# Router of a mixture-of-experts step: three of five row-tile shifts moved from VectorE to GpSimd

## The chip, the cores and the metric

The kernel runs on one core of one Trainium2 chip. The metric is the device time of one execution in microseconds (us); lower is better. A launch is one program on that one core, and nothing is shared with other cores.

## The reference, cut to what matters

One trunk layer is computed for 640 tokens (128 of context, 512 latent) with D_MODEL = 1024: modulated norm, one wide input projection, an RG-LRU and an attention branch, a merge, a gated residual, and then the part around which this case turns, the mixture of experts:

```
h = rms_norm(x, norm_g[1]) * (1 + sc2) + sh2            # sh2: the shift, one row for context, one for latent tokens
scores = sigmoid(h @ w_router)                          # 640 x 16
sel    = scores + router_bias, in 4 groups of 4
group  = argmax over groups of (sum of the group's two best)
idx    = the two best experts of that group;  w = their scores, normed to sum 1
y      = sum over the two experts e of w_e * (silu(h @ Wg[e]) * (h @ Wu[e])) @ Wd[e]
x      = x + g2 * y
```

## The kernel before, in words

**Stages.** The profile has three of them that matter here. Up to about 785 us TensorE works through 80 weight tiles of the projections. From there to about 816 us lies the router. From 816 us to about 1130 us the experts run, then a short tail adds the rows up, norms and stores them. Matrix products are made in three passes (high times high, high times low, low times high parts of fp32 values), which is why every weight has a Hi and a Lo tile.

**The router stage.** The modulated rows exist as columns in `xa` (channel by token) without the shift. They are needed twice. The logits come from products with the router's weights, with the shift's share added afterwards. The rows themselves are turned by TensorE (`to_rows`, L1048, forty 128x128 transposes in ten groups of four), evicted by ScalarE with the factor of the norm (`rows`, L1473) into `hrow`, five tiles of 128 tokens x 1024 channels, and then the shift row is added in place: `shifted(t)` on VectorE, L2006, one instruction of 128x1024 fp32 for each tile. `shb` holds the two shift rows spread over all partitions; SP loads it beforehand (semaphore `h2_pre`). SP writes each shifted tile to DRAM (`h2d`, called h_rows in the trace, L580), in order of t, each after its own wait for `slot_ok`, and right behind them on the same queue comes the load of the gate weights of expert 1.

**The order of VectorE's work.** It is written out by hand. VectorE makes the ranks (`pair_eq`, `pair_gt`, `in_rank`), the group choice (`gscore`, `r5`, `gtmp`, `ing`), the one-hot `ohsH` for TensorE (L2032), then positions, and at last `ohP` and `ohV` (L2083, L2085), from which TensorE makes the list of tokens of each slot (`idxI`, L2088). Between small instructions that depend on each other the five additions are placed as fill: tiles 0 and 1 after `top2` (L2008), tiles 2 and 3 after the first maximum of the group scores (L2019), tile 4 after the one-hot planes (L2035). `seq.last()` is a wait of VectorE for its own previous instruction.

**Who needs the results.** TensorE waits for `ohsH` at L1057, makes ranks across tokens, turns the residual rows of `x1` (`to_rows(1, ...)`, first four groups before the token list, six after it), and waits for all their evictions (`tr_ev`) before the first expert. ScalarE evicts those rows into `x1t` (L1475); between group four and five it makes the high part of the first up weights. GpSimd waits for `idxI` and for all five DRAM writes (`hrow_out`), then gathers the rows of the first expert tiles by an indirect DMA (L675). `x1t` and `shb` share memory: the last two tiles of `x1t` lie where `shb` lay.

**GpSimd.** Up to about 772 us it makes the low parts of the projection weights (L639, 128x1024, two inputs from SBUF); then it makes two small constants, and nothing more until the gathers. In the tail it multiplies three of the five tiles of summed rows by the gate (`gated`, L713).

Of the kernel before, what the change touches and what calls it, by code (L numbers as in the profile page):

```python
# [22 lines left out]
ALU = mybir.AluOpType  # L23
# [9 lines left out]
TT = T // P  # L33
# [73 lines left out]
HIGH_AT = (0, 3, 7, 11)  # L107
OUT_BANK = (2, 6, 4, 0, 2)
GATED_DVE = 2
ADA_ORDER = (4, 5, 6, 7, 0, 1, 2, 3)  # L110
SPANS = ((0, 0, NP), (1, NP, T))
XN = 3
# [2 lines left out]
def build(nc, xT, cT, w_ada, w_ada_late, b_ada, norm_g, final_g, wtiles, par_in, pack, biasd, w_router, r_bias,  # L115
# [112 lines left out]
    hrow = region(h0 + 4 * KT * T)("hrow", [TT, D])  # L228
# [56 lines left out]
    shb = region(x1t_at + 4 * (TT - 2) * D)("shb", [2, D])  # L285
# [22 lines left out]
    def C(name):  # L308
        a, n = CAT[name]
        return cst[:, a:a + n]  # L310
# [15 lines left out]
    pool_done, act_small, dve_small = sem("pool_done"), sem("act_small"), sem("dve_small")  # L326
# [15 lines left out]
    Wg0_in, sh_mm, sh_ok, h2_pre = sem("Wg0_in"), sem("sh_mm"), sem("sh_ok"), sem("h2_pre")  # L342
    tr_mm, tr_ev, slot_ok = sem("tr_mm"), sem("tr_ev"), sem("slot_ok")
# [107 lines left out]
    def _(sp):  # L451
# [124 lines left out]
        for g in range(2):  # L576
            sp.dma_start(g2d[g * KT:(g + 1) * KT, :], g2T[g:2 * KT:2, :]).then_inc(gb_in, 16)
        for t in range(TT):
            sp.wait_ge(slot_ok, t + 1)
            sp.dma_start(h2d[t * P:(t + 1) * P, :], hrow[:, t, :]).then_inc(hrow_out, 16)  # L580
        load(0, 1, 1)
        for x in (1, 2):
# [44 lines left out]
    def _(pool):  # L627
# [29 lines left out]
        low(N1 + N2 + N3 - 1, 1)  # L657
        nc.gpsimd.memset(onesH[:], 1.0).then_inc(ones_ok, 1)
        nc.gpsimd.tensor_copy(triH[:], C("tri")).then_inc(ones_ok, 1)

        pool.wait_ge(idx_ok, 1)
        pool.wait_ge(hrow_out, 16 * TT)
# [21 lines left out]
                gather(2 * j + 4 + b, b)  # L684
        seq.leave(more + (E // 2 - 2))
        seq.step(nc.gpsimd.tensor_copy(group2[:], groupI[:, bass.ds(2 * more + (E - 2), 2)]))
        pool.wait_ge(slot_ok, TT + 1)
        pool.wait_ge(zero_row, 16 * (SPILL + 3))
        pool.wait_ge(gb_in, 32)
        seq.last()  # L690
# [504 lines left out]
    def _(act):  # L1195
# [258 lines left out]
        def weights_high(x, t):  # L1454

            act.wait_ge(W_in[x], 16 * (t + 1))
            wait(act, W_mm[x], t)
            for k in range(0, KT, 4):
                A(W_hi[x][:, k:k + 4], Wraw[x][:, k:k + 4], ACT.Copy).then_inc(W_hi_ok[x], 1)  # L1459
# [7 lines left out]
        def rows(half, groups):  # L1467
            for gi in groups:
                g, o = 2 * TT * half + gi, gi % 2 * 512
                act.wait_ge(tr_mm, g + 1)  # L1470
                y = PS[:, (2, 3, 6, 7)[g % 4], :]
                if half == 0:
                    x = A(hrow[:, gi // 2, o:o + 512], y, ACT.Copy, scale=rs5[:, gi // 2:gi // 2 + 1])  # L1473
                else:
                    x = A(x1t[:, gi // 2, o:o + 512], y, ACT.Copy)  # L1475
                x.then_inc(tr_ev, 1)

        rows(0, range(2 * TT))
        rows(1, range(4))
        weights_high(1, 0)  # L1480
        rows(1, range(4, 2 * TT))

        def h_high(t, b):
# [76 lines left out]
    def _(dve):  # L1560
# [442 lines left out]
        def shifted(t):  # L2003

            dve.wait_ge(tr_ev, 2 * (t + 1))
            v.tensor_tensor(hrow[:, t, :], hrow[:, t, :], shb[:, min(t, 1)], ALU.add).then_inc(slot_ok, 1)  # L2006

        st(v.scalar_tensor_tensor(top2[:], in_rank[:], 1.5, sel[:], ALU.is_lt, ALU.mult))  # L2008
        shifted(0)
        shifted(1)  # L2010
        seq.last()
        gs = gscore[:].rearrange("p t g -> p (t g)")
        st(v.tensor_reduce(gs, top2[:].rearrange("p t (g x) -> p (t g) x", x=4), AX, ALU.add))
# [3 lines left out]
            return a.unsqueeze(2).broadcast_to([P, TT, n])  # L2017

        st(v.tensor_reduce(r5[0][:], gscore[:], AX, ALU.max))  # L2019
        shifted(2)  # L2020
        shifted(3)
        seq.last()
        st(v.tensor_tensor(gtmp[:], gscore[:], b3(r5[0][:], SP_G), ALU.is_equal))
# [224 lines left out]
        def summed(t):  # L2248

            dve.wait_ge(oc_mm, t + 1)  # L2250
            if t < GATED_DVE:
                dve.wait_ge(gg_ok, t + 1)
            else:
                dve.wait_ge(pool_done, t - GATED_DVE + 2)
            a = OUT_BANK[t]
            v.tensor_tensor(xo[t][:].rearrange("p (h c) -> p h c", h=2), PS[:, a:a + 2, :],  # L2256
                            G[t][:].rearrange("p (h c) -> p h c", h=2), ALU.add).then_inc(x2_ok, 1)
# [117 lines left out]
```

## Time and profile before

| what | value |
|---|---|
| median of 3 runs | 1166.7 us |
| lowest, highest | 1163.7, 1167.03 us |
| the profiled execution, its own time | 1171.21 us |
| its span, first to last instruction | 1169.3 us |
| mean granted clock of TensorE | 0.983 |
| busy: PE, PEld, DVE, ACT, POOL | 96%, 89%, 77%, 58%, 24% |

The span is one execution, and lies 1.9 us below that execution's own time. In the profile PE is TensorE, PEld its weight loads, DVE VectorE, ACT ScalarE, POOL GpSimd and SP the engine that issues most DMAs. A busy PE in these pages includes the modelled end of each matmul. A group of rows gives start, duration, engine, line, operation, tiles and count; the rest is said where the rows stand.

### The profile page before, as it was taken

How to read it: one execution, taken by the hardware profiler on the slowest of the kernel's cores; microseconds unless marked ns; L12 is line 12 of the kernel's file. 1: busy time of each engine (PE TensorE's matmuls, PEld its weight loads, DVE VectorE, ACT ScalarE, POOL GpSimd, SP SyncE). 2: the span in 40 equal slices, each digit the busy share in tenths (PEclk: the TensorE clock that was granted, in tenths of full speed). 3: DMA queues.
4: the chain of work that ended last, by engine and by line, in shares of the span. 5: the costliest groups of instructions: out<-in, count | busy, mean ns of one | idle time of the engine just before them, and what ended most of it. 6: DMA issues, size and time to landing. Idle time of an engine off the chain costs nothing.

```text
span 1169.3 us, 20318 instructions
## 1 busy us (share of the span) xinstructions
PE 1125.9 (96%) x7300; PEld 1039.9 (89%) x7300; DVE 901.4 (77%) x1267; ACT 680.1 (58%) x1041; POOL 283.9 (24%) x148
## 2 busy tenths in 40 slices
PE   8999999999999999899999999996999999999996
PEld 7899999999999998899999999995788888888874
DVE  5739797877969796967666646638899999899986
ACT  3565766666665856742222222436588778787853
POOL 2232212221222121133333332211112101012045
PEclk9999999999999999999999999996999999999998
DMA  9338322212121221124444445618899999999987
GB/s 373 139 100 226 113 73 69 71 53 85 58 72 51 81 70 52 42 92 149 143 145 145 145 149 183 235 33 319 314 360 420 428 413 414 420 406 421 418 307 192
DMA packets 54877, 233.27 MB, mean 199 GB/s; under 512 B 5369, under 2 KB 22049, under 8 KB 46369
## 3 DMA queue, kind: packets, MB, share of 16 engines
q1 hardware_dynamic: 50352, 216.27, 49.3%
q0 software_dynamic: 4320, 15.73, 4.2%
q8 instruction: 31, 0.51, 0.2%
q10 hardware_dynamic: 144, 0.52, 0.1%
q14 instruction: 30, 0.24, 0.1%
HBM read 211.50 MB, written 21.00 MB: 199 GB/s over the span
## 4 chain that ended last, share of the span: by engine, by line
PE 50%; DVE 3%; DMA 2%; issue 1%; POOL 1%; ACT 1%; ACTq 0%; DVEq 0%; POOLq 0%
PE PS L1087 23%; PE PS L823 22%; PE PS L1077 1%; DMA slot_rows<-Ys 1%; PE PS L993 1%; DMA G<-slot_rows,slotI 1%; POOL G L699 1%; PE PS L1100 1%; DVE hrow L2006 0%; PE PS L1048 0%; DVE xo L2256 0%; DVE WgLo L2144 0%; DVE yo L2266 0%; PE PS L937 0%; PE PS L972 0%
## 5 line engine op out<-in xcount | busy, mean ns | idle before, releaser
L639 POOL TENSOR_TENSOR wLo<-wRaw,wHi 128x1024 fp32r<-128x1024 f32 x80 | 205.0, 2562 | 532.6 <-ACT wHi L1212 517.0
L823 PE MATMUL PS<-hHi,wHi 128*128 128x320 f32 x880 | 279.8, 318 | 1.0 <-issue 0.6
L823 PE MATMUL PS<-hLo,wHi 128*128 128x320 f32 x880 | 272.2, 309 | 0.0
L823 PE MATMUL PS<-hHi,wLo 128*128 128x320 f32 x880 | 272.1, 309 | 0.0
L823 PEld LDWEIGHTS PS<-hHi,wHi 128*128 128x128 f32 x880 | 166.2, 189 | 1.8 <-issue 1.2
L823 PEld LDWEIGHTS PS<-hLo,wHi 128*128 128x128 f32 x880 | 166.0, 189 | 0.0
L823 PEld LDWEIGHTS PS<-hHi,wLo 128*128 128x128 f32 x880 | 165.6, 188 | 0.0
L1826 DVE SCALAR_TENSOR_TENSOR acc<-adaL,csil,acc 128x512 f32<-128x512 f32 x112 | 101.1, 961 | 9.8 <-DMA adaL<-in_w_ada_late 9.2
L1212 ACT ACTIVATE wHi<-wRaw 128x1024 fp32r<-128x1024 f32 x78 | 82.1, 1052 | 30.8 <-PE PS L823 29.4
L2144 DVE TENSOR_TENSOR WgLo<-Wg,WgHi 128x2048 fp32r<-128x2048 f32 x34 | 76.4, 2288 | 12.6 <-ACT WgHi L1459 12.6
L2144 DVE TENSOR_TENSOR WdLo<-Wd,WdHi 128x2048 fp32r<-128x2048 f32 x34 | 76.4, 2288 | 11.7 <-ACT WdHi L1459 11.6
L2144 DVE TENSOR_TENSOR WuLo<-Wu,WuHi 128x2048 fp32r<-128x2048 f32 x36 | 80.7, 2284 | 1.0 <-ACT WuHi L1459 1.0
L1681 DVE TENSOR_TENSOR PtLo<-PS,PtHi 128x384 fp32r<-128x384 f32 (+1 forms) x80 | 39.7, 496 | 53.6 <-ACT PtHi L1264 53.5
L1459 ACT ACTIVATE WgHi<-Wg 128x2048 fp32r<-128x2048 f32 x34 | 63.3, 1909 | 15.6 <-DMA Wg<-in_experts 13.7
L1331 ACT ACTIVATE Sb<-Sb,nmax 128x384 f32<-128x384 f32 (+1 forms) x80 | 45.0, 564 | 46.6 <-DVE nmax L1704 46.5
L667 POOL COPY idxc<-idxI 128x1 int32 (+1 forms) x16 | 19.8, 1239 | 214.6 <-PE PS L1077 214.6
L1692 DVE TENSOR_SCALAR Sb<-Sb,prec 128x384 f32<-128x384 f32 (+1 forms) x80 | 70.6, 924 | 1.4
L1264 ACT ACTIVATE PtHi<-PS 128x384 fp32r<-128x384 f32 (+1 forms) x80 | 35.5, 444 | 57.6 <-PE PS L903 57.0
L1459 ACT ACTIVATE WuHi<-Wu 128x2048 fp32r<-128x2048 f32 x36 | 66.8, 1907 | 3.5 <-DMA Wu<-in_experts 2.2
L1459 ACT ACTIVATE WdHi<-Wd 128x2048 fp32r<-128x2048 f32 x34 | 63.1, 1906 | 0.2 <-DMA Wd<-in_experts 0.2
L1087 PE MATMUL PS<-WgHi,hSH 128*128 128x512 f32 x144 | 56.9, 395 | 2.2 <-DVE WgLo L2144 1.3
L1087 PE MATMUL PS<-WuHi,hSH 128*128 128x512 f32 x144 | 57.8, 402 | 0.0
(380 smaller groups left out, 2871.4 us busy)
## 6 DMA issues: line engine op xcount, KB each, us to landing
wRaw<-in_wtiles SPq DMA_DIRECT2D x80, 512.0 KB, 3.7
Wu<-in_experts SPq DMA_DIRECT2D x18, 2048.0 KB, 9.6
Wg<-in_experts SPq DMA_DIRECT2D x18, 2048.0 KB
Wd<-in_experts SPq DMA_DIRECT2D x17, 2048.0 KB
adaL<-in_w_ada_late SPq DMA_DIRECT2D x32, 512.0 KB, 4.2
ada<-in_w_ada SPq DMA_DIRECT2D x8, 1024.0 KB, 17.8
slot_rows<-Ys SPq DMA_DIRECT2D x15, 512.0 KB, 10.6
slot_rows<-tab SPq DMA_DIRECT2D x12, 512.0 KB
```

The costliest lines, as they stand in the source:

```text
L639: nc.gpsimd.tensor_tensor(wLo[b][:], wRaw[b][:], wHi[b][:].bitcast(F32), ALU.subtract).then_inc(w_lo, 1)
L667: seq.step(nc.gpsimd.tensor_copy(idxc[b][:], idxI[:, bass.ds(t, 1)]))
L823: r = mm(PS[:, bank, 0:HALF], w[:, k, :], x[:, k, cols], start=(k == 0 and w is wHi[b] and x is xh), stop=(k == KT - 1 and w is wLo[b]))
L1087: x = mm(out, lhs[l][:, k, :], rhs[r](k)[:, cols], start=(k == 0 and l == r), stop=(k == n - 1 and l == 1))
L1212: A(wHi[b][:], wRaw[b][:], ACT.Copy).then_inc(w_hi, 1)
L1264: A(PtHi[:, 0:nt, hh * P:(hh + 1) * P], PS[:, 6, 0:nt * P].rearrange("p (t q) -> p t q", q=P), ACT.Copy).then_inc(pt_hi, 1)
L1331: A(Sb[(blk + b) % 2][hh][:, 0:w], Sb[(blk + b) % 2][hh][:, 0:w], ACT.Exp, scale=-1.0, bias=nmax[hh][:], accum_out=psumr[:, hh:hh + 1]).th ...
L1459: A(W_hi[x][:, k:k + 4], Wraw[x][:, k:k + 4], ACT.Copy).then_inc(W_hi_ok[x], 1)
L1681: v.tensor_tensor(PtLo[:, 0:nt, cols], PS[:, 6, 0:nt * P].rearrange("p (t q) -> p t q", q=P), PtHi[:, 0:nt, cols].bitcast(F32), ALU.subtra ...
L1692: v.tensor_scalar(x, x, prec[:, hh:hh + 1], None, ALU.mult).then_inc(prob_ok, 1)
L1826: y = v.scalar_tensor_tensor(acc[:, g, :], w, c1, acc[:, g, :], ALU.mult, ALU.add)
L2144: y = v.tensor_tensor(W_lo[x][:, k:k + 4], Wraw[x][:, k:k + 4], W_hi[x][:, k:k + 4].bitcast(F32), ALU.subtract)
```

## The change

A constant says how many tiles GpSimd shifts. GpSimd adds the shift to tiles 0, 1 and 2, each as soon as both of its halves are evicted, and counts them on `pool_done`, which already stands at 1 from an earlier memset. VectorE keeps tiles 3 and 4 at the places where they were. SP waits for `pool_done` for the first three DRAM writes and for `slot_ok` for the other two; the counts of later waits on both semaphores are adapted. ScalarE gets one new wait, for all three GpSimd additions, before it writes the later rows of `x1t`.

```diff
+SHIFT_POOL = 3
@@ sp: writes of the shifted rows
         for t in range(TT):
-            sp.wait_ge(slot_ok, t + 1)
+            if t < SHIFT_POOL:
+                sp.wait_ge(pool_done, t + 2)
+            else:
+                sp.wait_ge(slot_ok, t - SHIFT_POOL + 1)
             sp.dma_start(h2d[t * P:(t + 1) * P, :], hrow[:, t, :]).then_inc(hrow_out, 16)
@@ gpsimd: behind the two constants
+        pool.wait_ge(h2_pre, 48)
+        for t in range(SHIFT_POOL):
+            pool.wait_ge(tr_ev, 2 * (t + 1))
+            nc.gpsimd.tensor_tensor(hrow[:, t, :], hrow[:, t, :], shb[:, min(t, 1)], ALU.add).then_inc(pool_done, 1)
 
         pool.wait_ge(idx_ok, 1)
         pool.wait_ge(hrow_out, 16 * TT)
@@
-        pool.wait_ge(slot_ok, TT + 1)
+        pool.wait_ge(slot_ok, TT - SHIFT_POOL + 1)
@@ scalar
         rows(1, range(4))
         weights_high(1, 0)
+        act.wait_ge(pool_done, SHIFT_POOL + 1)
         rows(1, range(4, 2 * TT))
@@ vector
         st(v.scalar_tensor_tensor(top2[:], in_rank[:], 1.5, sel[:], ALU.is_lt, ALU.mult))
-        shifted(0)
-        shifted(1)
         seq.last()
@@
         st(v.tensor_reduce(r5[0][:], gscore[:], AX, ALU.max))
-        shifted(2)
         shifted(3)
         seq.last()
@@ vector, tail
-                dve.wait_ge(pool_done, t - GATED_DVE + 2)
+                dve.wait_ge(pool_done, SHIFT_POOL + t - GATED_DVE + 2)
```

## Rows read from the trace of the kernel before

**Rows 1.** Chain that ended last, 789 to 803 us: start us, us, what

```profile
795.85 2.27 DVE hrow L2006 x2
...
798.47 2.27 DVE hrow L2006 x2
...
802.08 1.22 DVE hrow L2006
```

**Rows 2.** Waits, 796 to 818 us: total us, times, longest us

```profile
PE PS L1057 <- DVE ohsH L2032: 5.5, 1, 5.5
```

**Rows 3.** Stretches: us, busy PE, PEld, DVE, ACT, POOL, PEclk, DMA share, GB/s

```profile
850.00:900.00 50.00, 50.00 (x240) 41.61 (x239) 46.22 (x29) 41.20 (x31) 6.61 (x5) 1.00 0.98 399
```

**Rows 4.** Timeline of VectorE, 793 to 801 us

```profile
793.23 0.49 DVE L1989 TENSOR_TENSOR pair_eq<-sel 128x320 f32<-128x320 f32 x1
793.63 0.48 DVE L1990 TENSOR_TENSOR pair_gt<-sel 128x320 f32<-128x320 f32 x1
...
795.08 0.49 DVE L1999 TENSOR_REDUCE in_rank<-pair_gt 128x80 f32<-128x320 f32 x1
795.60 0.24 DVE L2008 SCALAR_TENSOR_TENSOR top<-in_rank,sel 128x80 f32<-128x80 f32 x1
...
798.03 0.23 DVE L2013 TENSOR_REDUCE gscore<-top 128x20 f32<-128x80 f32 x1
798.30 0.18 DVE L2019 TENSOR_REDUCE r<-gscore 128x5 f32<-128x20 f32 x1
...
800.65 0.17 DVE L2023 TENSOR_TENSOR gtmp<-gscore,r 128x20 f32<-128x20 f32 x1
```

**Rows 5.** Timeline of ScalarE, 791 to 811 us

```profile
791.62 6.10 ACT L1473 ACTIVATE hrow<-PS,rs 128x512 f32<-128x512 f32 x10
...
810.91 0.60 ACT L1475 ACTIVATE x1t<-PS 128x512 f32<-128x512 f32 x1 [0.79 <-PE PS L1048]
```

**Rows 6.** GpSimd's line L713: duration ns min/median/max, first and last start

```profile
L713 POOL TENSOR_TENSOR G<-G,g2b x3: 2406/3336/3337, 1152.0 to 1157.7; 128x1024 f32<-128x1024 f32 x3
```

**Rows 7.** Timeline of GpSimd in the tail

```profile
1151.97 9.04 POOL L713 TENSOR_TENSOR G<-G,g2b 128x1024 f32<-128x1024 f32 x3 [3.80 <-DMA G<-slot_rows,slotI]
```

**Rows 8.** Timeline of VectorE in the tail

```profile
1153.54 1.93 DVE L2266 SCALAR_TENSOR_TENSOR yo<-xo,stat,fgb 128x1024 f32<-128x1024 f32 x1
...
1156.70 2.10 DVE L2266 SCALAR_TENSOR_TENSOR yo<-xo,stat,fgb 128x1024 f32<-128x1024 f32 x1
...
1163.34 1.28 DVE L2266 SCALAR_TENSOR_TENSOR yo<-xo,stat,fgb 128x1024 f32<-128x1024 f32 x1
```

**Rows 9.** Timeline of GpSimd, 745 to 777 us

```profile
753.76 2.41 POOL L639 TENSOR_TENSOR wLo<-wRaw,wHi 128x1024 fp32r<-128x1024 f32 x1 [7.05 <-PE PS L823]
```

**Rows 10.** Timeline of VectorE, 745 to 777 us

```profile
754.23 2.62 DVE L1913 TENSOR_TENSOR sqS<-sqS,sqa 128x640 f32<-128x640 f32 x1
...
763.27 0.82 DVE L1913 TENSOR_TENSOR sqS<-sqS,sqa 128x640 f32<-128x640 f32 x1
```

**Rows 11.** Timeline of the SP queue: issues of the shifted tiles

```profile
797.01 6.64 SPq L580 DMA_DIRECT2D h_rows<-hrow  x5
```

**Rows 12.** Timeline of VectorE, the token list

```profile
809.97 0.18 DVE L2088 CAST idxI<-PS 128x26 int32<-128x26 f32 x1 [0.41 <-PE PS L1067]
```

**Rows 13.** Timeline of GpSimd, the first gather

```profile
810.45 1.14 POOL L675 DMA_INDIRECT hS<-h_rows,idxI  x1 [37.40 <-DVE idxI L2088]
```

**Rows 14.** Chain that ended last, 770 to 850 us, the second router half and first expert

```profile
809.93 5.15 PE PS L1048 x24
...
815.76 0.68 PE PS L1077 x4
...
817.83 4.61 PE PS L1087 x12
...
823.73 2.77 PE PS L1087 x12
```

**Rows 15.** Short stretches, columns as in rows 3

```profile
812.00:814.00 2.00, 2.00 (x11) 2.00 (x10) 2.00 (x2) 1.49 (x3) 2.00 (x1) 0.50 0.71 203
...
822.00:824.00 2.00, 2.00 (x22) 1.67 (x22) 2.00 (x2) 0.24 (x1) 0.20 (x1) 1.00 0.88 352
```

## The prediction, as put on record before the changed kernel was run

> **What bounds the kernel now.** I began with the page: TensorE is busy for 96% of the span, so time can only be won where TensorE stands still or where it waits for a chain of other engines. The view by stretches shows which stages leave no such place: between 850 and 900 us, as in the other stretches of the expert stage, TensorE is busy for all 50 of 50 us at a granted clock of 1.00 [rows 3]. A shift in time of the start of that stage is therefore passed on to the end unchanged; nothing in it can win back or swallow a few us. Then I read the waits around the router: TensorE waits 5.5 us for `ohsH` of VectorE [rows 2]. The chain that ended last says what VectorE does in that time: from about 789.7 to 809.6 us it runs nearly without a gap through VectorE, and the five shifts stand in it, two pairs of 2.27 us and a single one of 1.22 us [rows 1]. So VectorE's queue bounds this stage, and each us taken from it before 809.6 us is a us of the kernel, if nothing takes its place.
>
> **What is removed.** Three of the five additions leave VectorE. I take the saving from starts, since neighbours overlap a little. `top` starts at 795.60 and `gscore`, which depends on it, at 798.03, so with two shifts between them the step is 2.43 us [rows 4]. Without them it is what dependent neighbours need, `top`'s 0.24 plus about 0.03, as from `gscore` at 798.03 to `r` at 798.30 [rows 4]. That saves 2.43 - 0.27 = 2.16 us. From `r` at 798.30 to `gtmp` at 800.65 are 2.35 us with two shifts [rows 4]; one of the two goes, half of 2.27 us [rows 1], or 1.13 us. Sum: 3.29 us off the path. Tiles 3 and 4 stay at their places.
>
> **What is added on GpSimd.** Three additions 128x1024 fp32 with both inputs in SBUF. The nearest rows are L713, the same shape, types and in-place form: 2.41 us at the least and 3.34 us for the other two [rows 6]; the low part of a weight tile, also 128x1024, took 2.41 us [rows 9]. The first can start once ScalarE has evicted two of the ten halves, which start at 791.62 and take 6.10 us for all ten, about 0.6 us each [rows 5]: at about 792.9 us. The second and third tile are ready at about 794.1 and 795.3 us, so the three follow each other without a gap of their own.
>
> **What GpSimd's work does to VectorE.** This is where the case is decided, since from 793 us on VectorE runs exactly the chain that bounds. At 753.76 us GpSimd starts a 128x1024 operation of 2.41 us, to 756.17 us; VectorE starts `sqS<-sqS,sqa`, two SBUF inputs, at 754.23 us, and it takes 2.62 us instead of the 0.82 us of the same line at 763.27 us [rows 9, 10]. It ends at 756.85 us, 0.68 us after GpSimd's end: it stood still until GpSimd was done and then ran its own time less 0.14 us of lead-in. The tail shows the same with a queue on both sides: GpSimd's three additions take 9.04 us in place of 3 x 2.41 = 7.23 us [rows 6, 7], while VectorE's `yo<-xo,stat,fgb`, again two SBUF inputs, takes 1.93 and 2.10 us in place of 1.28 us [rows 8]. Its first ends at 1155.47 us, its second at 1158.80 us [rows 8]: one GpSimd and one VectorE operation alternate with a period of 3.33 us. Less VectorE's own 1.28 us plus some 0.03 us between neighbours, a GpSimd addition puts 2.0 us into VectorE's chain; the first pair (rows 9 and 10: 2.62 - 0.82 = 1.80 us after a start 0.47 us late, so 2.27 us in all) puts the upper end at about 2.3 us. I take 2.1 us.
>
> From 792.95 us VectorE's next operations are `sel`, `pair_eq`, `pair_gt`, the product of `pair_eq` with a constant and the sum into `pair_gt`: all with two SBUF inputs, starting every 0.4 to 0.5 us [rows 4]. I therefore expect: first GpSimd addition 792.9 to 795.4, `pair_eq` to about 795.7, second to about 798.0, `pair_gt`, third to about 800.3, and only then the rest. The waits add 3 x 2.1 = 6.3 us; the bounds are 3 x 2.0 = 6.0 and 3 x 2.41 = 7.2 us, the latter if nothing of a hold hides behind VectorE's lead-in. Only a reduction, which has one input, could run beside GpSimd, `in_rank` of 0.49 us [rows 4]; by this order it comes after the third addition. If the order slips by one, 0.5 us are hidden.
>
> The Trainium skill, "SBUF — State Buffer", section "Who interferes with whom", says that a VectorE instruction with two SBUF inputs and a GpSimd instruction that reads SBUF exclude each other for the whole of whichever began first. The trace agrees, with the 2.62 us beside 0.82 us [rows 10]. Its section "A bandwidth-pool intuition that's wrong" gives about 115 ns from the release to the go-ahead of the other side in another pair of operations; an estimate with that would be 3 x (2.41 + 0.12) = 7.6 us, and the time 1171.0 us.
>
> **Sum on the path.** 6.35 us in (2.1 each, rounded up for the first, which also catches the start of `sel`) less 3.29 us out is +3.06 us, taken as +3.1 us, on the start of `ohsH` and on everything behind.
>
> **What lies beside it and costs nothing.** *SP's queue:* the five issues now run from 797.01 to 803.65 us and end with VectorE's fifth tile [rows 11]. Tiles 0 to 2 leave GpSimd at about 795.4, 798.0 and 800.3 us, before VectorE's tile 3 (about 803.8 us) and tile 4 (about 806.4 us), so SP's last issue and the weight load of expert 1 behind it are set by VectorE as before and move by the same 3.1 us. *GpSimd's queue:* it stands free from 772 us to the first gather at 810.45 us, 37.40 us idle [rows 13], so 7 us in it delay nothing. *The gather's second wait,* for the DRAM writes: the fifth is issued about 6 us before `idxI` is there (803.6 against 809.97 us) [rows 11, 12], and both move together. *ScalarE's new wait:* it stands in front of the eviction at 810.91 us [rows 5], the third addition ends some 10 us earlier; if that cover went, the six evictions behind it and then TensorE's first expert would wait. *Later waits with adapted counts* are met long before. *Six pairs of transposes and evictions* after the token list, 5.15 us [rows 14], start after it and move along.
>
> **TensorE's clock.** The clock stands at 0.50, the lower of its two levels (1.2 of 2.4 GHz), at 812 to 814 us, after TensorE had stood still for the 5.5 us of rows 2, and at 1.00 at 822 to 824 us [rows 15]. The first twelve expert matmuls take 4.61 us, a later twelve at full clock 2.77 us [rows 14]: 1.84 us is what the low level costs there. The 24 transposes, 5.15 us at the low level, are bounded by ScalarE's 6 x 0.6 = 3.6 us at the high one: 1.5 us. TensorE's pause becomes 3.1 us longer, and it is already at the low level afterwards; I take no change, with +1.8 us and -3.3 us as the bounds.
>
> **Forecast.** The profiled execution took 1171.21 us, 4.5 us above the median of 1166.7 us; its successor would be 1174.3 us, and the median 1166.7 + 3.1 = **1169.8 us**, 0.27% slower. A difference of about 0.3% (3.5 us) is what a measurement of this kernel can tell from no change, and the three runs shown spread over 3.3 us; so this forecast lies just inside.
>
> **Rivals.** *Full hold (slower):* at each of the three hand-overs, 793 to 801 us, VectorE loses the whole 2.41 us [rows 9], with nothing hidden by lead-in; 7.23 - 3.29 = +3.9 us, 1170.6 us. It decides over "no change" once an addition costs more than (3.5 + 3.29) / 3 = 2.26 us. For it: the 2.27 us worked out from rows 9 and 10; against: the period of the tail. Chance 0.20. *Side by side (faster side):* the two engines don't hinder each other for such small operations, because VectorE's next operation is back before GpSimd takes its turn; then -3.3 us, 1163.4 us. For it: no row shows instructions of 0.2 to 0.5 us against a queue on GpSimd; against: every pair with two SBUF inputs that I read. Chance 0.10. *Clock:* 1.8 us on top, 1171.6 us, or 3.3 us off, 1166.5 us; chance 0.15, half and half. *The moved work isn't on the path,* as something else, such as the gather, sets the end: 1166.7 us or a little less; against it stands the gapless chain; 0.05. My forecast has 0.50, and its own range is 1168.6 to 1171.0 us, about a third of it beyond +3.5 us.
>
> **Chances.** Slower: 0.18 from the forecast, 0.20 and 0.08 from full hold and clock, 0.46. Within 0.3%: 0.32 + 0.05 + 0.07 + 0.03 = 0.47. Faster: 0.05 + 0.02 = 0.07. The range of 1165.0 to 1173.0 us leaves out the side-by-side case and takes in both clock cases and the spread of the runs.
>
> **What the new profile would show.** Right: GpSimd's three additions start near 792.9 us and last until about 800 us, the later ones with durations above 2.4 us; `pair_eq` and `pair_gt` last over 2 us each in place of 0.5 us; `ohsH` starts near 804.6 us in place of 801.5 us; TensorE's wait at L1057 is near 8.6 us; the expert stage is the same, 3.1 us later. Wrong: VectorE's small operations keep 0.5 us while GpSimd runs (then side by side); `ohsH` is 3 us late but the end is not, which would be the clock; or the gather starts later than `idxI` allows.

## The result and the profile after

The changed kernel took 1171.51 us in the median (1166.73 to 1173.72 us), the kernel before, in the same session, 1166.91 us (1163.7 to 1169.22 us). The two medians are 4.6 us apart. The ratio worked out from all timed runs is 1.0037 with a 95% interval of 1.0027 to 1.0047: slower by 4.3 us, between 3.2 and 5.5 us. The forecast was 1169.8 us, the range 1165.0 to 1173.0 us.

| what | before | after |
|---|---|---|
| median | 1166.91 us | 1171.51 us |
| span of the profiled execution | 1169.3 us | 1171.1 us |
| mean granted clock of TensorE | 0.983 | 0.984 |
| reciprocal of the scores to `idxI` | 17.98 us | 21.03 us |
| reciprocal of the scores to the first expert matmul | 25.84 us | 29.40 us |

The two spans differ by less than the medians do, because in the profile after the router happens to start earlier: VectorE's reciprocal of the scores stands at 789.86 us, before at 791.99 us. Positions in the two traces must therefore not be subtracted; the distances of the last two lines are what can be compared. I call the distance from the reciprocal to `idxI` the chain from here on. The reciprocal in VectorE's timeline, first before, then after:

```profile
791.99 0.65 DVE L1979 RECIPROCAL sc<-sc 128x80 f32<-128x80 f32 x1
```

```profile
789.86 0.65 DVE L1988 RECIPROCAL sc<-sc 128x80 f32<-128x80 f32 x1
```

VectorE's timeline after, 790 to 811 us. The columns are start, duration, engine, line, operation, tiles, sizes and count.

```profile
791.09 2.53 DVE L1998 TENSOR_TENSOR pair_eq<-sel 128x320 f32<-128x320 f32 x1
793.55 2.64 DVE L1999 TENSOR_TENSOR pair_gt<-sel 128x320 f32<-128x320 f32 x1
796.11 2.62 DVE L2001 TENSOR_TENSOR pair_eq<-pair_eq,cst 128x320 f32<-128x320 f32 x1
798.77 0.49 DVE L2005 TENSOR_TENSOR pair_gt<-pair_gt,pair_eq 128x320 f32<-128x320 f32 x1
...
799.81 0.24 DVE L2017 SCALAR_TENSOR_TENSOR top<-in_rank,sel 128x80 f32<-128x80 f32 x1
800.09 0.23 DVE L2020 TENSOR_REDUCE gscore<-top 128x20 f32<-128x80 f32 x1
800.36 0.17 DVE L2026 TENSOR_REDUCE r<-gscore 128x5 f32<-128x20 f32 x1
...
801.58 0.17 DVE L2029 TENSOR_TENSOR gtmp<-gscore,r 128x20 f32<-128x20 f32 x1
...
810.89 0.18 DVE L2094 CAST idxI<-PS 128x26 int32<-128x26 f32 x1 [0.41 <-PE PS L1075]
```

GpSimd's timeline of the same stretch.

```profile
790.88 7.50 POOL L667 TENSOR_TENSOR hrow<-hrow,shb 128x1024 f32<-128x1024 f32 x3 [19.53 <-ACT hrow L1481]
811.37 1.14 POOL L683 DMA_INDIRECT hS<-h_rows,idxI  x1 [12.98 <-DVE idxI L2094]
```

The two rows of before between those of [rows 4], which the bill needs too:

```profile
794.04 0.48 DVE L1992 TENSOR_TENSOR pair_eq<-pair_eq,cst 128x320 f32<-128x320 f32 x1
794.55 0.49 DVE L1996 TENSOR_TENSOR pair_gt<-pair_gt,pair_eq 128x320 f32<-128x320 f32 x1
```

Here both sides of the bill can be read, against [rows 4]. Three VectorE instructions that took about half a us now take 2.5 to 2.6 us, one for each addition of GpSimd, and the fourth takes 0.49 us, since it starts at 798.77 us and GpSimd is done at 790.88 + 7.50 = 798.38 us. From start to start, `pair_eq` to `pair_gt` is 2.46 us (before 0.40), `pair_gt` to the product 2.56 us (0.41), the product to the next 2.66 us (0.51): 2.06 + 2.15 + 2.15 = 6.36 us in. Out: `top` to `gscore` is 0.28 us in place of 2.43 us, `r` to `gtmp` 1.22 us in place of 2.35 us, together 3.28 us. That leaves +3.08 us, and the chain from the reciprocal to `idxI` is 3.05 us longer.

The waits after, 796 to 822 us. The columns are total us, times, longest us.

```profile
PE PS L1065 <- DVE ohsH L2038: 8.1, 1, 8.1
PE PS L1085 <- DMA hS<-h_rows,idxI: 2.0, 1, 2.0
```

TensorE's wait for `ohsH` is 8.1 us in place of 5.5 us [rows 2]. The second line is a wait of 2.0 us for the first gather. The chain that ended last shows the gather too, and the first group of twelve expert matmuls:

```profile
811.37 5.41 DMA hS<-h_rows,idxI
...
819.26 5.16 PE PS L1095 x12
```

The first twelve took 5.16 us in place of 4.61 us [rows 14]. From `idxI` to the first expert matmul it is 819.26 - 810.89 = 8.37 us, in place of 817.83 - 809.97 = 7.86 us, so behind the chain 0.51 + 0.55 = 1.06 us more were lost in this one execution. Of the 2.0 us of waiting only some 0.2 us are a loss: TensorE's 24 transposes in front of it took 4.25 us in place of 5.29 us, and it began to turn the gathered rows 6.02 us behind `idxI` in place of 5.79 us. The stage after that is the same: TensorE is busy throughout at the granted clock of 1.00 [rows 3].

```profile
850.00:900.00 50.00, 50.00 (x236) 41.48 (x236) 46.78 (x31) 40.59 (x29) 5.08 (x6) 1.00 0.99 399
```

### The profile page after: what moved, and what is told of

Read it like the earlier page. It is cut to its first block, busy times and chain, and to the rows that moved or that the text cites. A ratio compares the mean times of both kernels' runs of the same rounds, so it can differ in the third digit from the quotient of the medians.

```text
span 1171.1 us, 20320 instructions
## 1 busy us (share of the span) xinstructions
PE 1123.5 (96%) x7300; PEld 1037.5 (89%) x7300; DVE 901.6 (77%) x1264; ACT 680.2 (58%) x1041; POOL 288.5 (25%) x151
## 4 chain that ended last, share of the span: by engine, by line
PE 49%; DVE 3%; DMA 2%; issue 1%; POOL 1%; ACT 1%; ACTq 0%; DVEq 0%; POOLq 0%
PE PS L1095 23%; PE PS L831 22%; PE PS L1085 1%; DMA slot_rows<-Ys 1%; PE PS L1001 1%; DMA G<-slot_rows,slotI 1%; POOL G L707 1%; PE PS L1108 1%; DMA hS<-h_rows,idxI 0%; DVE xo L2262 0%; DVE WgLo L2150 0%; DVE yo L2272 0%; PE PS L945 0%; PE PS L980 0%; PE PS L936 0%
## 5 line engine op out<-in xcount | busy, mean ns | idle before, releaser
L675 POOL COPY idxc<-idxI 128x1 int32 (+1 forms) x16 | 16.4, 1023 | 217.3 <-PE PS L1085 217.3
```

The costliest lines, as they stand in the source:

```text
L675: seq.step(nc.gpsimd.tensor_copy(idxc[b][:], idxI[:, bass.ds(t, 1)]))
```

## The experiments

Three questions were open. Is it GpSimd's reading of SBUF that holds VectorE, or only the time that passes? Does the lengthened chain explain the whole loss? And what would the move have brought if nothing were held? In the table below, "chain" is the distance defined above, "to expert" the distance from the reciprocal to the first expert matmul, and "row writes" the median time from issue to landing of the five DRAM writes of `hrow`. All three come from one profiled execution; the ratio comes from timed runs and is against the kernel before on the same chip.

| kernel | ratio [95%] | chain us | to expert us | row writes us |
|---|---|---|---|---|
| before | 1 | 17.98 | 25.84 | 3.0 |
| after | 1.0037 [1.0027, 1.0047] | 21.03 | 29.40 | 3.4 |
| e1: no GpSimd additions | 1.0002 [0.9987, 1.0016] | 14.84 | 25.53 | 9.0 |
| e2: memsets instead | 0.9997 [0.9981, 1.0014] | 14.84 | 25.56 | 6.5 |
| e3: before + filler | 1.0026 [1.0012, 1.0040] | 21.13 | 28.16 | 2.8 |
| e4: accumulating DMA | 1.0106 [1.0086, 1.0126] | 12.56 | 36.28 | 12.2 |
| e5: no additions, load behind the rows | 1.0043 [1.0027, 1.0058] | 14.85 | 27.36 | 8.8 |
| e6: PSUM operands, 3 on GpSimd | 1.0016 [1.0002, 1.0029] | 18.34 | 26.18 | 4.7 |
| e7: PSUM operands, 2 on GpSimd | 1.0012 [1.0000, 1.0024] | 18.30 | 26.05 | 3.2 |
| e8: 1 on GpSimd | 1.0013 [1.0002, 1.0023] | 18.89 | 26.46 | 2.8 |
| e9: PSUM operands by a copy, 2 on GpSimd | 0.9992 [0.9978, 1.0007] | 16.25 | 24.18 | 4.4 |
| e10: no additions, loads behind the gather | 1.0055 [1.0035, 1.0075] | 14.84 | 22.49 | 3.3 |
| e11: copies instead | one execution, 1167.8 us | 17.11 | 25.04 | 6.3 |
| e12: PSUM by a copy, load behind the gather | 1.0005 [0.9988, 1.0021] | 16.25 | 24.14 | 4.3 |

### Nothing on GpSimd (e1)

GpSimd only counts; tiles 0 to 2 go to DRAM without their shift.

```diff
-            nc.gpsimd.tensor_tensor(hrow[:, t, :], hrow[:, t, :], shb[:, min(t, 1)], ALU.add).then_inc(pool_done, 1)
+            pool.sem_inc(pool_done, 1)
```

> The changed kernel without the three GpSimd additions: the shift of tiles 0 to 2 is left out, and GpSimd only counts the tiles. Exclusion theory: pair_eq, pair_gt and the product fall back to 0.5 us each, and from the start of the reciprocal of sc to idxI the chain takes 17.98 - 3.29 = 14.7 us, against 18.0 before and 21.0 after; the time is 3.3 us below the kernel before, a ratio near 0.997. Rival, that the router's chain isn't what sets the start of the experts: the chain is as short, but the time is that of the kernel before, as the gather or the transposes take over.

The chain fell to 14.84 us, 3.14 us below before and 6.19 us below after: the additions themselves, and nothing else in the change, put the 6.2 us in. But the time did not follow. The ratio is 1.0002, with an interval that excludes a gain of more than 0.13% (1.5 us). The timelines of SP, VectorE and GpSimd show where most of the 3 us went:

```profile
790.65 7.58 SPq L584 DMA_DIRECT2D h_rows<-hrow  x5
...
805.97 4.49 DVE L2150 TENSOR_TENSOR WuLo<-Wu,WuHi 128x2048 fp32r<-128x2048 f32 x2
...
806.09 3.18 POOL L683 DMA_INDIRECT hS<-h_rows,idxI  x1 [34.58 <-DVE eI L2107]
```

The view of the tile `hrow`, its DMAs:

```profile
DMA to landing us min/median/max: 7.3/9.0/9.2
```

And the chain that ended last:

```profile
806.09 6.51 DMA hS<-h_rows,idxI
```

`idxI` is there at 789.70 + 14.84 = 804.54 us, but the gather starts only at 806.09 us, as the row writes, which took 3.0 us before, now take 9.0 us. They were issued from 0.95 us behind the reciprocal on, in place of 5.02 us [rows 11], into queues still full with the weights of the first expert. By its delay the gather comes 0.12 us behind VectorE's `WuLo`, which has two SBUF inputs, and its own instruction takes 3.18 us in place of 1.14 us [rows 13]; the same happens in the next experiment (3.25 us, 0.05 us behind `WuLo`). All in all "to expert" is only 0.31 us shorter than before. A second limit lies close behind VectorE's chain.

### Memsets in place of the additions (e2)

The time on GpSimd stays (six memsets of `hrow` tiles, which leave zeros in place of tiles 0 to 2), the reading goes.

```diff
-            nc.gpsimd.tensor_tensor(hrow[:, t, :], hrow[:, t, :], shb[:, min(t, 1)], ALU.add).then_inc(pool_done, 1)
+            nc.gpsimd.memset(hrow[:, t, :], 0.0).then_inc(pool_done, 1)
+            pool.wait_ge(pool_done, 2 * t + 2)
+            nc.gpsimd.memset(hrow[:, t, :], 0.0).then_inc(pool_done, 1)
```

> The changed kernel with two fills of 128x1024 by GpSimd for each of tiles 0 to 2 in place of the addition (the rows are overwritten by zeros, so the shift and the rows of three tiles are left out). GpSimd is busy at the same place but reads nothing from SBUF. Exclusion by reads: VectorE's pair_eq, pair_gt and product stay at 0.5 us, chain 14.7 us, time as without the additions (ratio near 0.997). Rival, that any GpSimd instruction on SBUF holds VectorE up, or that GpSimd's semaphore traffic does: they last over 1 us each and the chain is longer than 16 us.

GpSimd's and VectorE's timelines:

```profile
790.37 0.95 POOL L667 MEMSET hrow<- 128x1024 f32 x1 [19.03 <-ACT hrow L1483]
```

```profile
790.60 0.49 DVE L2000 TENSOR_TENSOR pair_eq<-sel 128x320 f32<-128x320 f32 x1
```

`pair_eq` runs wholly inside the first memset and takes its 0.49 us. Six memsets from 790.37 to 796.13 us add nothing: the chain is 14.84 us, as with an empty GpSimd. A GpSimd instruction that only writes doesn't hold VectorE. The ratio, 0.9997 [0.9981, 1.0014], repeats that 3.14 us off the chain bring nothing that shows at the end.

### Copies in place of the additions (e11)

```diff
-            nc.gpsimd.tensor_tensor(hrow[:, t, :], hrow[:, t, :], shb[:, min(t, 1)], ALU.add).then_inc(pool_done, 1)
+            nc.gpsimd.tensor_copy(hrow[:, t, :], shb[:, min(t, 1)]).then_inc(pool_done, 1)
```

> The changed kernel with GpSimd copying the shift row over each of tiles 0 to 2 in place of adding it (one SBUF input; the rows of three tiles are lost). Theory: what excludes is that GpSimd reads SBUF at all, so pair_eq and its neighbours wait for each copy to its end, however long it lasts, and the chain is 14.85 us plus about three times the copy less 0.3 us. Rival: only a GpSimd operation with two inputs excludes; then they stay at 0.5 us and the chain is 14.85 us.

GpSimd's and VectorE's timelines:

```profile
791.47 3.57 POOL L667 COPY hrow<-shb 128x1024 f32<-128x1024 f32 x3 [20.07 <-ACT hrow L1481]
```

```profile
791.68 1.21 DVE L1998 TENSOR_TENSOR pair_eq<-sel 128x320 f32<-128x320 f32 x1
792.81 1.32 DVE L1999 TENSOR_TENSOR pair_gt<-sel 128x320 f32<-128x320 f32 x1
794.05 1.32 DVE L2001 TENSOR_TENSOR pair_eq<-pair_eq,cst 128x320 f32<-128x320 f32 x1
```

One SBUF input on GpSimd's side is enough. A copy takes 1.19 us, and the chain is 17.11 - 14.84 = 2.27 us longer than with nothing, 0.76 us a copy. With the addition it is 6.19 us, 2.06 us each. So in these two cases the price goes with the length of GpSimd's instruction: 0.35 us less than its duration for the addition, 0.43 us less for the copy. The chain of the copies is read from one execution.

### The same time without GpSimd (e3)

The kernel before, with six more `pair_gt` instructions (3.1 us) in VectorE's chain.

```diff
+        for _ in range(6):
+            st(v.tensor_tensor(pair_gt[:], other, own, ALU.is_gt))
+            seq.last()
```

> The kernel before with six repeats of pair_gt on VectorE, each waiting for the one in front (same values, so the result is unchanged): about 6 x 0.52 = 3.1 us more in the chain, as much as the change put in, without any GpSimd work. If the whole cost of the change is the length of VectorE's chain: ratio 1.0027 to 1.004, as for the change, and the chain takes 21.1 us. If the change had a second cost that has to do with GpSimd (gather, DMA writes spread out), this one comes out at 1.0027 or below and the change lies clearly above it.

The chain is 21.13 us, the same as after, and the ratio 1.0026 with an interval of 1.0012 to 1.0040, or 1.4 to 4.7 us. A loss of 3.15 us in the chain does reach the end, though the interval leaves open whether all of it does. The change's 1.0037 [1.0027, 1.0047] overlaps with it: that GpSimd costs anything beyond the chain is not shown.

### The load held, to free the queues (e5)

As e1, and SP loads the next expert's gate weights only after the row writes have landed.

```diff
+        sp.wait_ge(hrow_out, 16 * TT)
         load(0, 1, 1)
```

> The kernel without the three additions (their shift left out) once more, with SP's gate-weight load of expert 1 held back until all five row writes have landed. Without this wait the chain to idxI was 3.2 us shorter and the time unchanged: the row writes took 7 to 9 us to land in place of 3, the gather was issued 1.1 us late, then lasted 3.2 us beside VectorE's WuLo and landed after 6.5 us in place of 4.9. If the load of 2 MB behind the rows is what slows their landing, the rows land in 3 to 5 us, the gather starts 0.3 us behind idxI, and the ratio is near 0.997. If the two weight loads in front of the rows (issued at 784 us) are what slows them, landing stays above 6 us for the first rows, but the fifth, issued near 798 us, still lands by 803 us: again 0.997 to 0.998. If the ratio stays at 1.000, the limit is the transposes and evictions of TensorE and ScalarE.

The row writes still take 7.1 to 9.0 us, so it is not the load behind them that delays them; what stands ahead is left, and e10 tries that. And the held load now meets the gather:

```profile
797.97 7.10 DMA h_rows<-hrow
...
805.95 8.53 DMA hS<-h_rows,idxI
```

The gather lands after 8.53 us (6.51 us in e1), and the ratio is 1.0043. This experiment moved the collision and didn't take it away.

### The loads held behind the gather (e10)

As e1, with two loads of weights held until the first gather has landed: one of those ahead of the row writes (the down weights of expert 0, now behind them), and the one behind.

```diff
         load(1, 0, 0)
-        load(2, 0, 0)
...
             sp.dma_start(h2d[t * P:(t + 1) * P, :], hrow[:, t, :]).then_inc(hrow_out, 16)
+        sp.wait_ge(hs_in[0], 16)
+        load(2, 0, 0)
         load(0, 1, 1)
```

> The kernel without the three additions (their shift left out), with SP's down-weight load of expert 0 and gate-weight load of expert 1 both held back until the first gather has landed. If the queue of weight bytes in front of the rows is the second limit of this stage, the five row writes land in about 3 us each, GpSimd's gather starts 0.3 us behind idxI and lands in 5 us, and TensorE turns the gathered rows 5 to 6 us behind idxI in place of 8.2 and 10.0 us; the ratio is 0.997 unless the held loads then make ScalarE wait, which would show as its waits for Wd and Wg before 830 us. If the landing stays above 6 us, the bytes are not the cause.

The row writes land in 3.3 us again and the gather in 4.99 us, and "to expert" is 22.49 us, 3.35 us below before:

```profile
805.02 4.99 DMA hS<-h_rows,idxI
```

So the second limit is the bytes of weights ahead of the rows in the DMA queues (holding the load behind them alone, in e5, left the row writes at 8.8 us): with the down weights held, the gather starts at 805.02 us, 0.47 us behind `idxI`, which is ahead of `WuLo` at 806.01 us, and its instruction takes 1.15 us. The held weights are missed later, though. The waits of ScalarE and TensorE:

```profile
ACT WdHi L1468 <- DMA Wd<-in_experts: 8.7, 1, 8.7
...
PE PS L1096 <- DVE WgLo L2151: 9.0, 1, 9.0
```

The ratio is 1.0055. Neither the load held in e5 nor the two held here could be put off for free.

### Fewer tiles on GpSimd (e8)

`SHIFT_POOL = 1`, the other four on VectorE.

```diff
-SHIFT_POOL = 3
+SHIFT_POOL = 1
@@ vector, behind top2
+        shifted(1)
@@ vector, behind the first maximum
+        shifted(2)
         shifted(3)
```

> The changed kernel with one tile on GpSimd in place of three, the other four shifts on VectorE. By the length of the chain, one hold of 2.1 us in and one shift of 1.13 us out: chain about 19.0 us against 18.0 before and 21.0 with three; ratio near 1.001. If the cost lies in something that any use of GpSimd there brings once, chain or time come out as with three, ratio 1.003.

The chain is 18.89 us: +0.91 us for one tile, +3.05 us for three, so about +1.0 us for each. One instruction is held, `pair_eq`:

```profile
791.26 2.54 DVE L1998 TENSOR_TENSOR pair_eq<-sel 128x320 f32<-128x320 f32 x1
793.73 0.48 DVE L1999 TENSOR_TENSOR pair_gt<-sel 128x320 f32<-128x320 f32 x1
```

Per tile, VectorE saves its 1.1 us and pays 2.1 us. The ratio of 1.0013 is in proportion, though within its interval (0.2 to 2.7 us) it says little.

### Operands in PSUM (e6, e7)

If two SBUF inputs on VectorE's side are what excludes, an instruction with one input from PSUM should run beside GpSimd. A second copy of `sel`, the results of the comparisons, and the group scores go to PSUM, so that each ranking instruction reads at most one tile of SBUF. PSUM is free at this time.

```diff
+        st(v.tensor_tensor(selP, sc[:], rbias[:].unsqueeze(1).broadcast_to([P, TT, E]), ALU.add))
...
-        st(v.tensor_tensor(pair_eq[:], other, own, ALU.is_equal))
-        st(v.tensor_tensor(pair_gt[:], other, own, ALU.is_gt))
+        st(v.tensor_tensor(eqP, other, own, ALU.is_equal))
+        st(v.tensor_tensor(gtP, other, own, ALU.is_gt))
...
-        st(v.tensor_tensor(pair_gt[:], pair_gt[:], pair_eq[:], ALU.add))
+        st(v.tensor_tensor(pair_gt[:], gtP, pair_eq[:], ALU.add))
```

> The changed kernel with GpSimd's three additions as they are, but one operand of each of VectorE's ranking instructions moved from SBUF to PSUM (one instruction more, a second copy of sel), so that none from pair_eq to the one-hots has two SBUF inputs; only the two shifts left on VectorE have. Exclusion by the second SBUF input: pair_eq, pair_gt and the product last about 0.5 us each beside GpSimd; the wait moves to the shift of tile 3 (about 1.3 us, behind the second addition) and of tile 4 (about 1 us, behind the third); the chain from the reciprocal of sc to idxI takes about 17 us, and the ratio is 0.998 to 1.001. Rival, that any VectorE instruction on SBUF is held while GpSimd adds: pair_eq and its neighbours last over 2 us as in the changed kernel, chain 21 us, ratio 1.003.

> The same with two additions on GpSimd and the shifts of tiles 2, 3 and 4 on VectorE, all behind the one-hots, when GpSimd is done. If only two SBUF inputs exclude each other nothing waits: two additions of 1.13 us leave the chain, some 0.5 us come in for PSUM and the second sel, chain about 16.3 us, 1.5 to 2 us less than before, ratio 0.9985 if the rows land in time (SP's load stays right behind them). If the gather is late as it was without the additions, 1.000.

VectorE's timeline of e6 (three tiles on GpSimd):

```profile
788.53 2.42 DVE L1997 TENSOR_TENSOR PS<-sc,rbias 128x80 f32<-128x80 f32 x1
790.98 0.50 DVE L2004 TENSOR_TENSOR PS<-sel,PS 128x320 f32<-128x320 f32 x1
...
794.00 2.54 DVE L2021 TENSOR_TENSOR hrow<-hrow,shb 128x1024 f32<-128x1024 f32 x1
```

And its GpSimd:

```profile
788.44 7.01 POOL L667 TENSOR_TENSOR hrow<-hrow,shb 128x1024 f32<-128x1024 f32 x3 [19.05 <-ACT hrow L1481]
```

The comparisons, with `sel` from SBUF and its twin from PSUM, take 0.50 us in the midst of GpSimd's additions. What is held is exactly what still reads two SBUF tiles: the sum that I had added to make the twin (2.42 us for 128x80), and VectorE's own fourth tile (2.54 in place of 1.22 us). Chain 18.34 us, ratio 1.0016. With two tiles on GpSimd and VectorE's three behind the one-hots (e7) the added sum is again caught at 2.41 us, chain 18.30 us, ratio 1.0012.

### The twin made by a copy (e9)

As e7, but the twin is copied, which reads one tile.

```diff
-        st(v.tensor_tensor(selP, sc[:], rbias[:].unsqueeze(1).broadcast_to([P, TT, E]), ALU.add))
+        seq.last()
+        st(v.tensor_copy(selP, sel[:]))
```

> In the run with two additions and PSUM operands the ranking instructions lasted 0.5 us beside GpSimd as expected, but the one instruction that was new, the second sel (sc and rbias, two SBUF inputs), stood behind GpSimd's first addition for 2.4 us. Here the second sel is a copy of the first into PSUM: one SBUF input. By exclusion through the second input nothing in VectorE's chain waits any more: chain from the reciprocal to idxI 18.3 - 2.3 + 0.3 = 16.3 us, 1.7 us under the kernel before; ratio 0.9985 if the gather keeps up. If anything on SBUF is held, the copy lasts over 2 us and the chain stays near 18.3 us.

VectorE's and GpSimd's timelines:

```profile
789.37 0.24 DVE L1998 COPY PS<-sel 128x80 f32<-128x80 f32 x1
789.65 0.50 DVE L2005 TENSOR_TENSOR PS<-sel,PS 128x320 f32<-128x320 f32 x1
```

```profile
789.16 4.71 POOL L667 TENSOR_TENSOR hrow<-hrow,shb 128x1024 f32<-128x1024 f32 x2 [19.44 <-ACT hrow L1481]
```

Now nothing is held while GpSimd adds two tiles, and GpSimd isn't slowed either (4.71 us for two; three took 7.50 us after). The chain is 16.25 us, 1.73 us below before, and the first expert starts 1.66 us sooner. The ratio is 0.9992 with an interval of 0.9978 to 1.0007: clearly better than the change. It can't be told from the kernel before, nor from a gain of the whole 1.7 us, which would be 0.9985.

Does the expert stage pass the 1.7 us on? The last matmuls of that stage, the down products of the last expert, can be found in each profile. Their group shows count, durations in ns, and first and last start; first before, then e9:

```profile
L1087 PE MATMUL PS<-WgHi,aTH x8: 389/389/501, 1136.3 to 1141.2; 128*128 128x512 f32 x8
```

```profile
L1095 PE MATMUL PS<-WgHi,aTH x8: 387/389/496, 1130.7 to 1135.6; 128*128 128x512 f32 x8
```

With them each execution falls into pieces, all in us; the table has those of seven kernels, each from its one profiled execution. "Stage" runs from the end of the first twelve expert matmuls to the last start shown above, "reciprocal to last" from the reciprocal to the same start, and "tail" from there to the end of the span.

| kernel | first twelve | stage | reciprocal to last | tail |
|---|---|---|---|---|
| before | 4.61 | 318.8 | 349.2 | 28.1 |
| after | 5.16 | 318.8 | 353.3 | 27.9 |
| e1 | 5.49 | 319.0 | 350.0 | 29.0 |
| e2 | 5.49 | 319.3 | 350.3 | 28.6 |
| e3 | 3.03 | 318.7 | 349.9 | 29.1 |
| e9 | 4.52 | 318.8 | 347.5 | 30.0 |
| e12 | 4.58 | 319.5 | 348.2 | 25.9 |

In before, after, e3 and e9 the stage takes the same time whether it starts early or late: e9 comes to its last matmuls 1.7 us sooner than the kernel before, with nothing lost on the way, and the changed kernel 4.1 us later. (In e1 and e2 it takes 0.2 and 0.5 us more; e12 is the next experiment.) ScalarE waits 5.1 us for the weights of the last expert in e9 and 2.3 us before, but TensorE isn't held by it. In e9's execution the tail took 1.9 us more, where a DMA in the chain that ended last landed after 10.52 us in place of 9.37 us, first e9, then before:

```profile
1113.04 10.52 DMA slot_rows<-Ys
```

```profile
1118.29 9.37 DMA slot_rows<-Ys
```

The tail took from 25.9 to 30.0 us in all these kernels without following the chain (25.9 us in e12, whose chain is e9's), so these profiles don't show that it is a cost of e9.

### The same with the load behind the gather (e12)

In e9 TensorE still waits 1.1 us for the gather. Here the load behind the row writes waits for it.

```diff
+        sp.wait_ge(hs_in[0], 16)
         load(0, 1, 1)
```

> The version with two additions on GpSimd and PSUM operands, whose chain to idxI was 1.7 us shorter than before, lost part of that again: TensorE waited 1.1 us for the first gather, which landed after 6.0 us beside the gate-weight load of expert 1, and its ratio was 0.9992 [0.9978, 1.0007]. Here SP holds that load until the first gather has landed. If the load is what slows the gather: landing near 5 us, no wait of TensorE for it, ratio 0.998. The load is needed by ScalarE only near 822 us and should be there by then; if not, ScalarE's wait for Wg grows and the ratio is 1.000 or above. If the rest is the clock of TensorE, nothing changes against 0.9992.

The gather lands after 5.24 us (5.28 us in e9), so this load is not what slows it. TensorE's wait for it stays (0.97 us), and the load is missed at the start of expert 1: the chain that ended last has

```profile
828.58 10.09 DMA Wg<-in_experts
```

Ratio 1.0005 [0.9988, 1.0021], no gain over e9.

### The shift added by the DMA (e4)

SP first writes the shift rows into `h2d`, and GpSimd's queue adds the rows to them in DRAM; no engine adds anything.

```diff
+        for t in range(TT):
+            sp.dma_start(h2d[t * P:(t + 1) * P, :], shb[:, min(t, 1)]).then_inc(h2_pre, 16)
@@ gpsimd
-            nc.gpsimd.tensor_tensor(hrow[:, t, :], hrow[:, t, :], shb[:, min(t, 1)], ALU.add).then_inc(pool_done, 1)
+            nc.gpsimd.dma_start(h2d[t * P:(t + 1) * P, :], hrow[:, t, :], accum_op=ALU.add).then_inc(hrow_out, 16)
```

> No engine adds the shift: SP writes the shift row to DRAM for each token ahead of the router, and GpSimd issues one accumulating DMA of each unshifted tile onto it. All five additions leave VectorE's chain: about 18.0 - 5.6 = 12.4 us to idxI. If the accumulated writes have landed by then, the time is 5.6 us below the kernel before, ratio 0.995. If each takes over 5 us to land, the gather waits for the fifth, which is issued near 799 us, and the gain is 2 to 4 us; if they take over 12 us it is a loss.

From the list of DMA issues (KB each, median us to landing), the chain, and the stretch 796 to 804 us:

```profile
h_rows<-hrow POOLq DMA_DIRECT2D x5, 512.0 KB, 12.2
```

```profile
795.05 14.90 DMA h_rows<-hrow
810.81 12.07 DMA hS<-h_rows,idxI
```

```profile
796.00:804.00 8.00, 3.93 (x32) 3.60 (x31) 7.18 (x28) 6.46 (x8) 0.00 (x0) 0.73 1.05 209
```

An accumulating write of 512 KB lands after 12.2 us in the median, a plain one of before after 3.0 us, and one of e1, issued about as early behind the same loads, after 9.0 us. The DMA engines are busy for the whole stretch and move 209 GB/s, while in e1 they move 412 GB/s from 796 to 804 us, and in the expert stage 399 GB/s [rows 3]. The ratio is 1.0106: with VectorE's chain emptied of all five additions, the rows arrive too late.

## Why the prediction was right, and where it was not

**What bounds.** Right for a loss, wrong for a gain. That VectorE's chain bounds the router stage, and that time put into it reaches the end, is shown by e3. The sentence that failed is "each us taken from it before 809.6 us is a us of the kernel": e1 and e2 take 3.14 us off, and the first expert starts only 0.31 and 0.28 us sooner, since the row writes and the gather take over. The sentence on the expert stage, "nothing in it can win back or swallow a few us", is borne out: the stage takes 318.7 to 318.8 us before, after, in e3 and in e9, and 0.2 and 0.5 us more in e1 and e2. The DMA share of 0.98 beside TensorE's 50 of 50 us [rows 3], which I didn't weigh, cost no more than that.

**What is removed.** Forecast 3.29 us, measured 3.28 us; in e1 and e2 the chain is 3.14 us shorter than before.

**What GpSimd's work does to VectorE.** Forecast 3 x 2.1 us, taken as 6.35 us; measured 2.06, 2.15 and 2.15 us, 6.36 us together. The instructions held were `pair_eq`, `pair_gt` and the product, as listed, and the pattern was as read from the tail: one VectorE instruction passes between two of GpSimd. The full-hold rival, with 2.41 us each (7.23 us), is out as a mechanism, though its 1170.6 us is nearer to the time measured. So is the "side by side" rival, twice: the engines do exclude each other, and where they don't (e2) the 3.3 us don't reach the end. It would have been better priced near 1166.7 us than at 1163.4 us.

The Trainium skill, "SBUF — State Buffer", section "Who interferes with whom", has the rule of exclusion, and these runs agree with it where they touch it: an addition (2.53 us for a 0.49 us `pair_eq`) and a copy (1.21 us) on GpSimd exclude, a memset (0.49 us) doesn't, and a VectorE instruction with one input from PSUM is not held (0.50 us). The estimate from the 115 ns of its section "A bandwidth-pool intuition that's wrong" came to 7.6 us for three additions and 1171.0 us; in the chain 6.36 us were measured. Some 0.3 us of each addition don't show in VectorE's chain at all; the period of the two engines in the tail [rows 7, 8] had everything of that kind included, and came closer.

**What lies beside it.** SP's queue, GpSimd's queue and ScalarE's new wait cost nothing that any view shows; GpSimd was done at 798.38 us and stood idle for 12.98 us before the gather.

**The gather and the clock.** Here are the terms that were mis-sized. "Both move together" gave 0 for the gather, and "I take no change" 0 for the clock. In the one profile TensorE waited 2.0 us for the gather, of which some 0.2 us were lost, and `idxI` to the end of the first twelve matmuls took 1.06 us longer than before. The low level of the granted clock lasted a little longer, as a short stretch of after shows (columns as in [rows 15]):

```profile
822.00:824.00 2.00, 2.00 (x6) 1.61 (x5) 2.00 (x2) 0.93 (x1) 0.00 (x0) 0.52 0.95 383
```

Here the clock is still 0.52 up to 4.7 us behind the first expert matmul at 819.26 us; before it stood at 1.00 from 822 us on, 4.2 us behind the one at 817.83 us [rows 14, 15]. This lies inside the bound of +1.8 us that I gave. But among these kernels the first twelve matmuls take 3.0 to 5.5 us without a pattern that follows the chain (3.03 us in e3, whose chain is as long as the changed kernel's), so this is noise as much as a cost. The timed runs say the same: of the 34 of the kernel before that were timed beside e5, the six fastest (1163.0 to 1164.8 us) had a mean granted clock of 0.989 to 0.991, the six slowest (1168.5 to 1169.7 us) 0.984 to 0.987.

**Sum.** +3.1 us were forecast and +4.3 us (3.2 to 5.5 us) measured. The chain's 3.05 us lie just below that interval, and the filler, with the same chain, measured 1.4 to 4.7 us. In the profiled pair the pieces add up: 3.05 us of the chain, 0.51 us up to the first expert matmul and 0.55 us in the first twelve are 4.1 us at the last matmuls. In that of the filler, 0.7 us of its 3.15 us are left at the same place, as the way from `idxI` to the first expert matmul took 0.8 us less than before and the first twelve 1.6 us less; so one profile can't say what the clock costs on average. The range of 8 us would have held most rivals and no change at all as well; what bears the prediction out is the chain, not that the time fell inside. The clock rival's 1171.6 us is the size that was measured, but that the clock is the cause is not shown. Whether some 1 us comes from GpSimd's work in another way, or from the gather and the clock by chance, stays open: the two intervals overlap, and nothing I ran parts them.

## What to carry to other kernels

Before fill work goes from VectorE to an idle GpSimd, look at what VectorE runs in that time: if its instructions read two SBUF tiles, each GpSimd instruction that reads SBUF goes into VectorE's chain for nearly its whole length, and GpSimd's is twice as long (2.41 against 1.22 us), so the move costs about 1 us for each 1.1 us of work that it takes away. An operand in PSUM lifts this, if also the instruction that puts it there reads one SBUF tile only.

Price a delay and a saving on the path that bounds separately. The delay of 3.15 us reached the end; of the saving of 3.14 us only 0.3 us reached the next stage in the profile, because another path into the same stage (the row writes and the gather) lay close behind, and since the row writes, issued earlier, met fuller DMA queues: they took 9.0 us in place of 3.0 us. To see what a saving is worth, take the work out altogether first: here that gave 1.0002 [0.9987, 1.0016], and with it most of the answer to the idea of moving these three additions.

## What was unexpected of the hardware

- Accumulating DMA writes move about half the bytes per time of plain traffic here: 209 GB/s with the DMA engines busy throughout, against 412 GB/s in the same stretch of e1. 512 KB landed after 12.2 us, plain after 9.0 us in queues as full (e1) and 3.0 us before. They fill the queues for all others: the gather behind them took 12.07 us in place of 5.41 us in the changed kernel.
- GpSimd's time for 128x1024 fp32 depends on the inputs: memset 0.95, copy 1.19, addition 2.41 us (at 4.71 us for two).
- The gather's instruction on GpSimd is held by a two-input VectorE instruction too. In the kernel before, its second gather starts in the midst of the first `WuLo` of 128x2048 (2.28 us each) and takes 2.66 us; in e4, where `WuLo` is over by 807.71 us, it takes 0.99 us. The lines are `WuLo` and the second gather of before, then the second gather of e4:

```profile
811.44 4.49 DVE L2144 TENSOR_TENSOR WuLo<-Wu,WuHi 128x2048 fp32r<-128x2048 f32 x2
```

```profile
811.89 2.66 POOL L675 DMA_INDIRECT hS<-h_rows,idxI  x1 [0.30 <-DVE eI L2101]
```

```profile
812.17 0.99 POOL L680 DMA_INDIRECT hS<-h_rows,idxI  x1 [0.30 <-issue]
```

  That of before ends 0.83 us behind the end of the first `WuLo`. The gathers of e1, e2 and e5 that start inside a `WuLo` end 0.8 to 1.0 us behind its end, wherever in it they start. This is read from the traces; no edit took `WuLo` away.
- A tiny VectorE instruction suffers as much as a large one: 128x80 took 2.42 us in e6 in place of 0.24 us, ten times its length.
